# Sample attention of a decoder step on one NeuronCore, its key turning, sums and schedule rewritten

## The reference, cut

```python
H, HD = 16, 64                                  # heads, head size
past_k = cache_k[page_table].reshape(8, 4096, H, HD)
past_v = cache_v[page_table].reshape(8, 4096, H, HD)
keys = concatenate([past_k, k_new], axis=1)     # k_new: the 8 new tokens
vals = concatenate([past_v, v_new], axis=1)
z = einsum('bqhd,bkhd->bhqk', q, keys) * HD**-0.5 + bias      # float32
mask = kpos < qpos                              # strictly causal
log_beta = log_sigmoid(z)
log_keep = where(mask, log_beta - z, 0.0)       # = -softplus(z)
rest = cumsum(log_keep, axis=3, reverse=True) - log_keep      # over the keys behind
a = where(mask, exp(log_beta + rest), 0.0)
o = einsum('bhqk,bkhd->bqhd', a, vals)
```

## Time and profile before

| | us |
|---|---|
| median of 3 runs | 3756.63 (3754.12 to 3758.39) |
| the profiled execution | 3754.67 |
| its span | 3752.9 |
| `attend_sample`, from its first load to the first load of `attend_prompt` | 1492.58 to 2316.78 |

### The profile page before, as it was taken

How to read it: one execution, slowest core, us unless ns; L and a number is a source line. 1 busy time by engine, 2 the same in 40 slices (tenths; PEclk the granted TensorE clock), 3 DMA queues, 4 the chain that set the end, 5 groups by cost and what they waited for, 6 DMA issues and landing times. The chain is left out here.

```text
span 3752.9 us, 57991 instructions
## 1 busy us (share of the span) xinstructions
PE 3221.6 (86%) x20912; PEld 2726.6 (73%) x20912; DVE 1899.9 (51%) x3234; ACT 901.9 (24%) x1502; POOL 610.6 (16%) x528
## 2 busy tenths in 40 slices
PE   5655999999996979788888887888886899999997
PEld 1235999999986979555555554444484899999996
DVE  2566555555543121344444445888824555555554
ACT  0123000000011010333333344666614100000003
POOL 0002122222101111122222221000010222222210
PEclk8887999999998989899999998999998999999998
DMA  8702111111102210788888885000010211111101
GB/s 325 258 26 62 45 45 45 45 40 44 34 0 70 78 60 28 310 351 335 337 340 339 344 345 185 23 17 23 6 45 0 68 45 45 45 45 45 45 22 48
DMA packets 215604, 432.70 MB, mean 115 GB/s; under 512 B 13665, under 2 KB 130058, under 8 KB 212442
## 3 DMA queue, kind: packets, MB, share of 16 engines
q1 hardware_dynamic: 215521, 431.67, 31.6%
HBM read 417.92 MB, written 13.92 MB: 115 GB/s over the span
## 5 line engine op out<-in xcount | busy, mean ns | idle before, releaser
L84 PE MATMUL bank<-hi,mlp_uphi 128*128 128x364 f32 (+1 forms) x1536 | 506.8, 330 | 92.3 <-POOL mlp_uplo L697 92.3
L85 PE MATMUL bank<-lo,mlp_uphi 128*128 128x364 f32 (+1 forms) x1536 | 506.8, 330 | 0.0
L86 PE MATMUL bank<-hi,mlp_uplo 128*128 128x364 f32 (+1 forms) x1536 | 506.5, 330 | 0.0
L85 PE MATMUL bank<-mlp_flo,mlp_dnhi 128*128 128x364 f32 (+1 forms) x1536 | 504.8, 329 | 0.0
L84 PE MATMUL bank<-mlp_fhi,mlp_dnhi 128*128 128x364 f32 (+1 forms) x1536 | 504.7, 329 | 0.0
L86 PE MATMUL bank<-mlp_fhi,mlp_dnlo 128*128 128x364 f32 (+1 forms) x1536 | 504.7, 329 | 0.0
L307 DVE SCALAR_TENSOR_TENSOR x_t<-bank,mod,x_t 128x364 f32<-128x364 f32 (+1 forms) x432 | 245.4, 571 | 379.6 <-PE bank L86 377.3
L84 PEld LDWEIGHTS bank<-hi,mlp_uphi 128*128 128x128 f32 x1536 | 290.4, 189 | 93.4 <-POOL mlp_uplo L697 93.4
L697 POOL TENSOR_TENSOR mlp_uplo<-mlp_raw,mlp_uphi 128x1024 fp32r<-128x1024 f32 x64 | 162.1, 2535 | 825.5 <-ACT mlp_uphi L682 422.7
L85 PEld LDWEIGHTS bank<-lo,mlp_uphi 128*128 128x128 f32 x1536 | 290.5, 189 | 0.0
L86 PEld LDWEIGHTS bank<-hi,mlp_uplo 128*128 128x128 f32 x1536 | 290.4, 189 | 0.0
(11 more groups left out here) (254 smaller groups left out, 5626.8 us busy)
## 6 DMA issues: line engine op xcount, KB each, us to landing
sa_kpage<-in_cache_k SPq DMA_DIRECT2D x256, 512.0 KB, 6.4
sa_vpage<-in_cache_v SPq DMA_DIRECT2D x256, 512.0 KB, 6.0
mlp_raw<-in_w_up SPq DMA_DIRECT2D x64, 512.0 KB, 3.9
mlp_raw<-in_w_down SPq DMA_DIRECT2D x64, 512.0 KB, 3.4
w_raw<-in_w_ada SPq DMA_DIRECT2D x24, 1024.0 KB, 8.6
pm_wada<-in_w_ada SPq DMA_DIRECT2D x48, 512.0 KB, 5.4
kv_raw<-in_w_kv SPq DMA_DIRECT2D x8, 1024.0 KB, 5.6
x_rows<-in_x_prompt SPq DMA_DIRECT2D x1, 4096.0 KB, 13.4
```

Source lines behind the costliest of these rows:

```text
L84: pe.matmul(out, w_hi, x_hi, start=start, stop=False, skip_group_check=True)
L85: pe.matmul(out, w_hi, x_lo, start=False, stop=False, skip_group_check=True)
L86: return pe.matmul(out, w_lo, x_hi, start=False, stop=stop, skip_group_check=True)
```

## The change

All of it is in `attend_sample`, but for a constant and an address.

- **Key loads.** A page of keys is now written to 32 partitions only: page g of a unit goes to partitions 32g to 32g+31, as 4 rows of 4 KB in each (tokens j, 32+j, 64+j, 96+j on partition 32g+j). The value pages are loaded as before. Keys of a unit are asked for once all 4 turns of the unit two before are done (`turned`), and no longer page by page.
- **Turning.** DVE turns the keys in blocks of 32 by 32 (`dve.transpose`, 4 instructions of 128x1024 for each unit), from SBUF to SBUF. TensorE's 32 transposes and the 8 copies of ACT and DVE go. Two buffers `sa_kt`.
- **Scores.** After a block turn, partition 32g+r holds element r of half a head, for page g. The queries are laid block-diagonally (`sa_q`, 4 pages x 8 queries = 32 columns), so that one multiplication contracts over (page, half head): 32 multiplications of 128 columns in the place of 8 of 512. ACT adds the bias in 4 pieces of 128 columns.
- **Sums.** `c_run` is the running sum over pages, on DVE: 4 additions of 128 columns in a unit. TensorE needs 6 multiplications in the place of 10. POOL has only 4 instructions for each sequence.
- **Schedule.** The 64 units are one row, written out without loops on TensorE, ACT, DVE and POOL; sequence b+1 begins before b has ended. `Z`, `ZT` and `OA` have two banks each. TensorE: values of n-1, scores of n+1, turn the scores of n+1, sums of n. DVE: softplus, sums and split of n, then the key turns of n+2. SP keeps its loop.
- `CAP` in `attend_prompt` is another constant; `k.o_s` has its address by another name.

```diff
@@ attend_sample
+    UNITS, W = 8, 8 * DB
     with ExitStack() as ctx:
         o = k.HH_AT
-        k_t = k.at("sa_kt", [P, NC, 512], F32, o)
-        k_pages = [k.at("sa_kpage0", [P, 4, D], F32, o + 16384), k.at("sa_kpage1", [P, 4, D], F32, o + 51712)]
...
+        k_raw = [k.at(f"sa_kraw{s}", [P, 4, D], F32, o + 16384 * s) for s in range(2)]
+        k_t = [k.at(f"sa_kt{s}", [P, 4, D], F32, o + 32768 + 16384 * s) for s in range(2)]
...
-        Z, ZTS, OA = k.ps[3], [k.ps[4], k.ps[6]], k.ps[5]
-        ZN = [k.ps[5], k.ps[6]]
-        OT = [k.ps[6], k.ps[3]]
-        TURN_BANKS = [k.ps[0], k.ps[1], k.ps[2], k.ps[7]]
...
+        Z, ZT, OA = [k.ps[0], k.ps[1]], [k.ps[2], k.ps[3]], [k.ps[4], k.ps[5]]
+        ZN = OT = [k.ps[6], k.ps[7]]
...
+        EARLY_K, EARLY_V = 8, 2
...
-                        sp.wait_ge(k_turned, b * TURNS + (2 * (n + 25) if n < 8 else 2 * (n - 7) + TURNS))
-                        sp.dma_start(k_pages[u % 2][:, g, :], kc[bass.ds(page[n], 1), :, :].rearrange("n p d -> (n p) d")
+                        sp.wait_ge(turned, b * (4 * UNITS) + (4 * u - 4 + EARLY_K))
+                        sp.dma_start(k_raw[u % 2][32 * g:32 * g + 32, :, :],
+                                     kc[bass.ds(page[n], 1), :, :].rearrange("n (x j) d -> j (n x) d", j=32)
                                      ).then_inc(k_in[n % 8], 16)
                     for g in range(4 if u else 0):
                         n = 4 * (u - 1) + g
-                        sp.wait_ge(v_used, b * UNITS + (u + 6))
+                        sp.wait_ge(v_used, b * UNITS + (u - 2 + EARLY_V))
...
+            for s in range(2):
+                pool.memset(q_w[s][:, :, :, :], 0.0).then_inc(q_zeroed, 1)
...
+            pool.wait_ge(summed, 2)
+            for b in range(DB):
+                if b:
+                    pool.wait_ge(v_used, EARLY_V + UNITS * (b - 1) + 1)
+                mine = row_of[:, b:b + 1].to_broadcast([P, P])
+                pool.tensor_tensor(sp_b[:, :], sp_all[:, :], mine, ALU.mult).then_inc(new_own, 1)
+                pool.wait_ge(new_own, 2 * b + 1)
+                pool.tensor_tensor(pn_hi[:, :], sp_b[:, :], k.zeros[:, :], ALU.add).then_inc(new_own, 1)
+                pool.wait_ge(new_own, 2 * b + 2)
+                pool.tensor_tensor(pn_lo[:, :], sp_b[:, :], pn_hi[:, :].bitcast(F32), ALU.subtract).then_inc(new_ready, 1)
+                pool.tensor_tensor(att_b[:, :], att_all[:, :], mine, ALU.mult).then_inc(new_ready, 1)
...
-                for u in range(UNITS):
-                    keep(u, range(4))
-                    if u:
-                        weights(u - 1)
...
+            def softplus_of_negative(n):
+                for hb in range(4):
+                    cols = slice(P * hb, P * hb + P)
+                    if hb == 0:
+                        act.wait_ge(z_done, n + 1)
+                        act.wait_ge(zt_done, n)
+                    act.activation(z_rows[:, cols], Z[n % 2][:, cols], ACT.Identity, bias=bias_4[:, hb:hb + 1]
+                                   ).then_inc(z_kept, 1)
+                act.wait_ge(zt_done, n + 1)
+                act.wait_ge(c_done, 4 * n)
+                act.activation(flat, ZT[n % 2][:, :], ACT.Abs).then_inc(abs_done, 1)
+                act.wait_ge(abs_done, n + 1)
+                act.activation(flat, flat, ACT.Exp, scale=-1.0).then_inc(e_done, 1)
+                act.wait_ge(e_done, n + 1)
+                act.activation(flat, flat, ACT.Ln, bias=1.0).then_inc(l_done, 1)
+
+            act.wait_ge(bias_made, 4)
+            softplus_of_negative(0)
+            for n in range(W):
+                if n + 1 < W:
+                    softplus_of_negative(n + 1)
+                act.wait_ge(tri_done, n + 1)
+                if n:
+                    act.wait_ge(v_used, EARLY_V + n)
+                act.activation(att[:, :, :].rearrange("p g (h q) -> p h g q", h=H),
+                               ZT[n % 2][:, :].rearrange("p (h g q) -> p h g q", h=H, g=4), ACT.Exp).then_inc(a_done, 1)
...
+            def ready_queries(b, g):
+                if b == 0 and g == 0:
+                    dve.wait_ge(q_zeroed, 2)
+                if b >= 2:
+                    dve.wait_ge(z_done, UNITS * (b - 1))
+                for par in range(2):
+                    for half in range(2):
+                        src = 64 * par + 32 * half
+                        dve.tensor_copy(
+                            q_w[b % 2][32 * g:32 * g + 32, :, half, 8 * g:8 * g + 8]
+                            .rearrange("p (c r) q -> p r c q", r=2)[:, par, :, :],
+                            k.q_t[src:src + 32, :, TP + b * DS:TP + b * DS + DS]).then_inc(q_ready, 1)
+            for g in range(4):
+                ready_queries(0, g)
...
+            def turn_keys(n, x):
+                if n >= W:
+                    return
+                if x == 0:
+                    for g in range(4):
+                        dve.wait_ge(k_in[4 * (n % 2) + g], 16 * (n // 2 + 1))
+                    if n >= 2:
+                        dve.wait_ge(z_done, n - 1)
+                dve.transpose(k_t[n % 2][:, x, :], k_raw[n % 2][:, x, :]).then_inc(turned, 1)
...
+            for n in range(2):
+                for x in range(4):
+                    turn_keys(n, x)
...
+            for n in range(W):
+                b, u = divmod(n, UNITS)
+                flat = t[:, :, :, :].rearrange("p h g q -> p (h g q)")
+                dve.wait_ge(l_done, n + 1)
+                dve.scalar_tensor_tensor(flat, ZT[n % 2][:, :], 0.0, flat, ALU.max, ALU.add).then_inc(sp_done, 1)
+                dve.wait_ge(sp_done, n + 1)
+                if n:
+                    dve.wait_ge(lo_done, n)
+                for g in range(4):
+                    if g:
+                        dve.wait_ge(c_done, 4 * n + g)
+                        before = c_run[:, :, g - 1, :]
+                    elif u:
+                        before = c_run[:, :, 3, :]
+                    else:
+                        dve.wait_ge(new_ready, 2 * b + 1)
+                        before = sp_b[:, :].rearrange("p (h q) -> p h q", h=H)
+                    dve.tensor_tensor(c_run[:, :, g, :], before, t[:, :, g, :], ALU.add).then_inc(c_done, 1)
+                c_all = c_run[:, :, :, :].rearrange("p h g q -> p h (g q)")
+                dve.wait_ge(c_done, 4 * n + 4)
+                if n:
+                    dve.wait_ge(tri_done, n)
+                dve.tensor_copy(c_hi[:, n % 2, :, :], c_all).then_inc(hi_done, 1)
+                dve.wait_ge(hi_done, n + 1)
+                dve.tensor_tensor(c_lo[:, n % 2, :, :], c_all, c_hi[:, n % 2, :, :].bitcast(F32), ALU.subtract
+                                  ).then_inc(lo_done, 1)
+                for x in range(4):
+                    turn_keys(n + 2, x)
+                if u == 1 and b:
+                    finish(b - 1)
+                if 2 <= u < 6 and b + 1 < DB:
+                    ready_queries(b + 1, u - 2)
...
+            def scores(n):
+                b = n // UNITS
+                pe.wait_ge(turned, EARLY_K + 4 * n + 4)
+                if n >= 2:
+                    pe.wait_ge(z_kept, 4 * (n - 1))
+                if n % UNITS == 0:
+                    pe.wait_ge(q_ready, 16 * (b + 1))
+                for hb in range(4):
+                    for half in range(2):
+                        for c in range(4):
+                            h = 4 * hb + c
+                            last = pe.matmul(Z[n % 2][32 * c:32 * c + 32, P * hb:P * hb + P], q_w[b % 2][:, h, half, :],
+                                             k_t[n % 2][:, :, 64 * h + 32 * half:64 * h + 32 * half + 32],
+                                             start=(hb == 0 and half == 0), stop=(half == 1),
+                                             tile_position=(0, 32 * c), skip_group_check=True)
+                last.then_inc(z_done, 1)
+
+            def turn_scores(n):
+                pe.wait_ge(z_kept, 4 * n + 4)
+                if n >= 2:
+                    pe.wait_ge(a_done, n - 1)
+                for hb in range(4):
+                    last = pe.matmul(ZT[n % 2][:, P * hb:P * hb + P], z_rows[:, P * hb:P * hb + P], k.ident[:, :],
+                                     start=(hb == 0), stop=False, is_transpose=True, skip_group_check=True)
+                last.then_inc(zt_done, 1)
...
+            def subtract_sums(n):
+                b, u = divmod(n, UNITS)
+                zt = ZT[n % 2][:, :].rearrange("p (h r) -> p h r", h=H)
+                pe.wait_ge(lo_done, n + 1)
+                if u == 0:
+                    pe.wait_ge(new_ready, 2 * b + 1)
+                for half, new in ((c_hi, pn_hi), (c_lo, pn_lo)):
+                    pe.matmul(zt, k.neg_tri[:, :], half[:, n % 2, :, :], start=False, stop=False, skip_group_check=True)
+                    pe.matmul(zt[:, :, DS:32], k.neg_above[:, :], half[:, n % 2, :, 0:32 - DS], start=False, stop=False,
+                              skip_group_check=True)
```

(20 more changed lines are left out.)

307 lines of the change are left out of this document (86 added, 221 removed).

## The result

The changed kernel takes 4138.05 us (median of 4 runs, 4125.07 to 4143.81) where the kernel before takes 3756.43 us beside it. The ratio is 1.102, 95% interval 1.100 to 1.104: 10% slower, not the 4% of the forecast, and above its range (3990). The profiled execution has a span of 4137.1 us.

What follows compares the result with a forecast made beforehand. TensorE's order was taken to bound `attend_sample`, the DMAs close behind. From 1534.3, 62 key units at 9.75 and 61 value units at 5.09, plus the tail, put the stage's end 158.8 us later: 3915 us, range 3700 to 3990.

Steps and rivals of the forecast that it cites:

- The bound: `attend_sample`: TensorE's order sets the pace at 11.39 us a unit, DMAs close behind at 10.2.
- Engines: `attend_sample` after the change, work per unit: TensorE 6.5 us, DVE 8.1, ACT 3.6, none over 10.2.
- The ring of 9.9: `attend_sample`: chain through TensorE, ACT and DVE, from values and scores to weights with hand-overs, 9.9 us a unit.
- the ring rival: `attend_sample`: TensorE falls to 1.2 GHz, the engines' chain takes 15.3 us or more; 4020 us (3955 to 4150), chance 0.08.
- Keys at 215 GB/s: `attend_sample` key loads on 32 partitions: between 204 and 225, taken as 215 GB/s, 9.75 us a unit.
- The values keep 412: 5.09 us.: `attend_sample` value loads on 128 partitions stay at 412 GB/s, 5.09 us; with keys 14.8 us a unit.
- half hidden: `attend_sample`: DMA engines drift apart, keys at 290 GB/s, unit 12.3 us; 3758 us (3700 to 3882), chance 0.16.
- The row at 18 us: Earlier trace, sample rows on 64 partitions: 250 GB/s with engines busier than ever, evidence for slow key loads.
- The sum: `attend_sample`: 62 key units at 9.75 and 61 value units at 5.09 from 1534.3, last keys landing at 2449.3.
- Some 280 GB/s: Sign for the forecast: mid-stage windows of `attend_sample` with a DMA share near 1 and some 280 GB/s.
- Key loads that take longer to land than value loads: Sign for the forecast in `attend_sample`: key loads take longer from issue to landing than value loads; no size given.
- Units of 14 to 15 us: Sign for the forecast: units of `attend_sample` take 14 to 15 us, without a longer one at the sequence's end.

Runs made afterwards that it cites:

- values alone: Changed kernel with key pages loaded once in the stage's head and never again, value loads kept: 3510.5 us.
- keys alone: Changed kernel with value pages loaded once in the stage's head and never again, key loads kept: 3604.5 us.
- wide keys: Changed kernel with each key page loaded onto 128 partitions instead of 32, so scores are other numbers: 3674.9 us.
- the run with gathered keys: Changed kernel with keys brought by four GpSimd indirect loads a unit, each onto 128 partitions, everything computed: 3642.9 us, ratio to before 0.970.

## Why the prediction was wrong

*The bound.* Right: the DMAs were close behind TensorE, the change moved the pace to them, and DVE waits for `sa_kraw` as said.

*Engines.* Right, nearly term by term (DVE's 8.1 leaves out the copies of the queries, 0.4 us): turn 1.21 (1.23 forecast), scores 2.5 at full clock and 3.64 at half (2.9), bias 4 x 0.37 = 1.5 as the sum of its four pieces and 1.14 as they overlap (1.1), four additions 1.27 (1.1), DVE 7.9 a unit (8.1). The ring of 9.9 was if anything too long, since values alone ran at 8.2. The clock fell to 0.72 as the ring rival feared, but scores and values at 3.64 us don't fill an 18 us unit.

*Keys at 215 GB/s.* Right: 216 in the head, 218 alone. A bound drawn from short bursts on 64 partitions, held for a whole stage of keys alone.

*"The values keep 412: 5.09 us."* This is the step that failed, and all of it. By the issue at 1538.59 and the landing at 2673.18, 62 units of keys at 9.75 leave 530.1 us for 61 units of values, 8.69 us each: (8.69 - 5.09) x 61 = 220 us of the 224 that were missing (4.3 in the head, 3.8 of them from before the stage). That books the whole loss on the values. In the mixed queue no row tells one kind from the other, so what is shown is their sum, 18.2 us a unit in place of 14.8, and not the split. The row it stood on, 415 and 408 GB/s in the earlier trace rows, was measured with wide loads on both sides. I carried a rate from a stretch in which nothing narrow was in the queue into a queue half full of narrow loads, and gave the term one value where every other unknown had two ends. The rival "half hidden" let a mixture be better than the sum; none let it be worse. The opposite end, values as slow as keys (9.75), would have given 19.5 us a unit and some 4200 us, and a range drawn to it would have held the result.

*The row at 18 us.* The prediction says that the loads on 64 partitions in the earlier trace rows stood alone. For the sample rows that isn't so. SP issues them at 5.60 us, behind the 4 MB of prompt rows (5.16) and ahead of four weight loads of 1 MB (from 6.57), all of these on 128 partitions and in one queue. The row at 18 us was the middle of a mixture:

```profile
17.00:18.00 1.00, 0.00 (x0) 0.00 (x0) 0.00 (x0) 0.00 (x0) 0.00 (x0) 1.00 1.09 340
...
19.00:20.00 1.00, 0.00 (x0) 0.00 (x0) 0.00 (x0) 0.00 (x0) 0.00 (x0) 1.00 0.75 238
20.00:21.00 1.00, 0.83 (x4) 0.83 (x5) 0.00 (x0) 0.00 (x0) 0.00 (x0) 1.00 1.00 418
```

The three microseconds from 17 to 20 moved 0.83 MB, of which 0.26 were the sample rows: one behind the other, at 215 and 412 GB/s, they would be 2.6 us. It is small and short, but it was the one place in that trace that showed both kinds in one queue.

*The sum.* 62 x 9.75 + 61 x 5.09 is 915.0 us; the 815.0 is a slip of the pen, and 2449.3 is reckoned with 915.0, so that the forecast of 3915 stands as its terms give it.

*What a mixture does.* Shown: the loss needs narrow writes (wide keys: gone; narrow keys in the kernel before: there) and both kinds at once (keys alone 218, values among themselves 373 and more), and a second queue or an emptied one takes most of it away. How it comes about inside the DMA engines is argued only. In the trace the engines are busy nearly all the time (0.97) while they move 230 GB/s in place of 403: their packets take longer, and they don't stand for want of work. A picture that fits: with one queue in order, an engine that is through with its narrow share early starts on values, into partitions whose ways in the others' narrow writes still fill, while other ways stand idle. No row names an engine or a way in, so this stays open.

(The Trainium skill, SBUF — State Buffer, section "Door 1: The DMA port swizzle", says that 32 partitions reach 8 of 16 ports at 27.2 GB/s each, which gives 217.6, and the trace agrees, 218. By the same section one engine serves one port in a load of 128 partitions; no run here shows that. Had the two kinds shared all ports evenly, each port would carry 262 KB a unit, 9.6 us as an estimate from this page; the trace has 18.2.)

*The signs named beforehand.* DMA share near 1 and DVE's waits: right. "Some 280 GB/s": 230. "Key loads that take longer to land than value loads": wrong, both 23.9 us, because time to landing counts the queue ahead of a page, whatever kind it is. Kept apart, they did differ: windows of 219 and 373 GB/s. "Units of 14 to 15 us": 18.9 in the mean, from 12.7 to 23.2. "Without a longer one at the sequence's end": there is one of 22 to 27 us, but the one behind it takes 8 to 11, and the two together less than two ordinary ones, so nothing is lost at the ends, as said.

## What to carry to other kernels

A transfer's rate belongs to its company: before a rate from an old trace goes into a sum, ask whether what will stand beside it in the queue stood beside it there, and if not, give it two ends. Look at the number of partitions that a load writes to before anything it makes cheaper; here a layout that saved 3 us a unit on the engines (11.4 to 8.2) cost 8 on the loads (from 10.2, or 10.4 in the run with gathered keys, to 18.2). And where a layout needs rows from several pages, gather them for all partitions at once instead of loading a page into a corner.

## What the runs showed that was not expected

- Narrow and wide loads of the same size in one queue ran at 230 GB/s, less than one after the other (283 by 218 and 403), and hardly more than narrow ones alone.
- The loss came by the round of keys and values: 4.1 us for four pages and four, 3.8 for eight and eight.
- Gathers of 128 rows of 4096 bytes ran as fast as plain loads (403 GB/s in all, with half of the pages gathered), at 0.96 us of GpSimd each.
- 64 small multiplications of 32 columns cost TensorE only 1.30 us, but stretches of some 3 us without any named cause came with them.
- TensorE's granted clock, as a mean over the long windows, was 0.72 in the changed kernel, where TensorE is busy for 423 of 1000 us, and 1.00 with keys alone, where it is busy for 296 of 500. With gathered keys it was 0.93 at 300 of 500: the busy share alone doesn't tell it.
